# The last pair's drain, token tile 0 and the order of the output sums at the end of a decoder layer with MoE, on one core

## The reference

```python
x = x + g1[:, None, :] * (merged @ w_out[l])
h = modulate(rmsnorm(x, norm2[l]), sh2, sc2)
x = x + g2[:, None, :] * hier_moe(h, ...)
# hier_moe: each token goes to 2 of 32 experts, with weights e_w:
#   hid = silu(t @ w1) * (t @ w3) ; out += e_w * (hid @ w2)
```

## Time and profile before

| | us |
|---|---|
| median of 3 runs | 618.57 |
| lowest, highest | 617.46, 618.89 |
| profiled execution | 618.94 |
| its span | 617.1 |
| busy in the span: PE, DVE, ACT, POOL | 567.7, 303.4, 161.2, 118.8 |

### The profile page before, as it was taken

The page is one execution under the profiler, slowest core; times in us unless marked ns, Lnnn a source line. Parts: engine busy times, 40 slices in busy tenths (PEclk is TensorE's granted clock), DMA queues, the critical chain, the costliest instruction groups (busy, mean ns, idle before and its releaser), DMA issues.

```text
span 617.1 us, 7419 instructions
## 1 busy us (share of the span) xinstructions
PE 567.7 (92%) x2824; PEld 340.7 (55%) x2824; DVE 303.4 (49%) x579; ACT 161.2 (26%) x346; POOL 118.8 (19%) x162
## 2 busy tenths in 40 slices
PE   3889999999999999999999999999979868888894
PEld 1644787777666676788888864433323322233343
DVE  0228889556656466138854585432213202265147
ACT  3026040345333434346321301211112101112100
POOL 3022421089200002066000002111111101101000
PEclk9999999999999999999999999999989988889998
DMA  8996665520671507030697499999999999999963
GB/s 307 401 351 249 245 236 201 171 106 31 256 291 63 210 0 275 1 137 0 256 382 317 172 411 401 375 421 418 420 420 419 421 418 421 416 421 414 399 259 136
DMA packets 43768, 173.50 MB, mean 281 GB/s; under 512 B 6552, under 2 KB 6640, under 8 KB 32980
## 3 DMA queue, kind: packets, MB, share of 16 engines
q1 hardware_dynamic: 36288, 158.87, 65.0%
q0 software_dynamic: 5664, 12.51, 5.6%
q10 hardware_dynamic: 1780, 1.63, 0.8%
HBM read 164.86 MB, written 15.74 MB: 293 GB/s over the span
## 4 chain that ended last, share of the span: by engine, by line
PE 77%; DMA 11%; DVE 6%; issue 4%; SPq 1%; ACT 1%; POOL 0%; DVEq 0%; POOLq 0%; ACTq 0%
PE bank L1067 18%; PE bank L1104 8%; PE bank L724 5%; PE bank L726 5%; PE bank L725 5%; PE bank L713 4%; DMA late<-in_w_ada_dram 4%; DMA arena<-y_scratch 3%; DMA late<-in_w_in_dram 3%; PE bank L1035 2%; PE bank L717 2%; PE bank L719 2%; PE bank L907 2%; PE bank L718 2%; PE bank L909 2%
## 5 line engine op out<-in xcount | busy, mean ns | idle before, releaser
L1067 PE MATMUL bank<-arena,hT 128*64 128x512 f32 x320 | 79.7, 643 | 16.2 <-issue 15.3
L724 PE MATMUL bank<-hT_high,w_in_parts 128*128 128x512 f32 x160 | 66.3, 414 | 0.0
L726 PE MATMUL bank<-hT_high,w_in_parts 128*128 128x512 f32 x160 | 62.7, 392 | 0.0
L725 PE MATMUL bank<-hT_low,w_in_parts 128*128 128x512 f32 x160 | 62.4, 390 | 0.0
L1884 DVE SCALAR_TENSOR_TENSOR g1b<-g1b,bank 128x256 f32<-128x256 f32 x16 | 6.7, 421 | 108.2 <-ACT g1b L1407 108.2
L1067 PEld LDWEIGHTS bank<-arena,hT 128*64 128x64 f32 x320 | 24.8, 146 | 62.3 <-issue 61.3
L1067 PE MATMUL bank<-late,hT 128*64 128x512 f32 x160 | 37.9, 619 | 3.9 <-issue 3.9
L2219 POOL DMA_INDIRECT hT<-xn_scratch,gidx x14 | 15.9, 1134 | 110.4 <-PE bank L1035 94.4
L1413 ACT COPY g1b<-bank 128x256 f32<-128x256 f32 x16 | 6.0, 372 | 112.8 <-PE bank L1087 112.8
L1592 DVE TENSOR_REDUCE st<-bank 128x2 f32<-128x256 f32 (+3 forms) x16 | 13.2, 824 | 43.1 <-PE bank L750 43.1
L726 PEld LDWEIGHTS bank<-hT_high,w_in_parts 128*128 128x128 f32 x160 | 30.0, 188 | 6.7
(11 more groups left out here) (345 smaller groups left out, 1048.0 us busy)
## 6 DMA issues: line engine op xcount, KB each, us to landing
arena<-in_w_dram SPq DMA_DIRECT2D x48, 1024.0 KB, 23.7
late<-in_w_dram SPq DMA_DIRECT2D x28, 1024.0 KB, 26.7
late<-in_w_ada_dram SPq DMA_DIRECT2D x6, 2048.0 KB, 13.3
arena<-in_w_dram SPq DMA_DIRECT2D x24, 512.0 KB, 12.7
arena<-in_w_ada_dram SPq DMA_DIRECT2D x5, 2048.0 KB, 9.3
arena<-in_w_in_dram SPq DMA_DIRECT2D x4, 2048.0 KB, 7.5
late<-in_w_in_dram SPq DMA_DIRECT2D x4, 2048.0 KB, 15.8
y_scratch<-arena POOLq DMA_DIRECT2D x1, 4096.0 KB, 18.2
```

Source lines behind the costliest of these rows:

```text
L724: mm(bank[:, b, :], wH[:, b, k, :], hH[:, k, :], start=k == 0, stop=False)
L725: mm(bank[:, b, :], wH[:, b, k, :], hL[:, k, :], start=False, stop=False)
L726: last = mm(bank[:, b, :], wL[:, b, k, :], hH[:, k, :], start=False, stop=k == 7)
L1067: last = mm(bank[SLOTS * x:SLOTS * (x + 1), 2 + q % 2, :].rearrange("p (w f) -> p w f", w=2), xgT_of(q)[:, k, SLOTS * x:SLOTS * (x + 1)], ...
```

## The change

- SP reads the stored rows in the order of tiles 1, 0, 2, 3.
- In `step(15)` DVE now has only the first of tile 1's two sums. The first half of the last pair is drained behind it, then comes tile 1's second sum, then the second half's drain. Tile 2's two sums, before in `step(15)`, stand ahead of its first output now, as tile 3's do.
- DVE adds six outputs in the order n = 1, 5, 2, 6, 3, 7 (`OUT_ORDER`). Tile 0 (n = 0 and 4) is no longer among them: PE puts the residual rows into the two banks with an identity matrix (`first_tile`, one fp32 matmul of 512 columns for each half, opening the sum in the bank), and ACT copies the finished banks to `xs`, after which SP stores them.
- On PE the first of these matmuls stands in the middle of the last pair's `gate_up`, ahead of the wait for the second half of the weights. The second stands behind the last pair's `down`, and with it `spread(STORED, 4)`, which stood ahead of that `down`.
- The lines on `overflow` belong to a part that runs only where an expert has more than 64 tokens.

```diff
+        ROW_ORDER = (1, 0, 2, 3)
+        OUT_ORDER = (1, 5, 2, 6, 3, 7)
...
-            rows_of(range(TT))
+            rows_of(ROW_ORDER)
...
-            for n in range(2 * TT):
+            def store_out(n):
                 t, w = n % TT, slice(CH * (n // TT), CH * (n // TT + 1))
-                sp.wait_ge(out_ready, n + 1)
                 sp.dma_start(out_v[t][:, w], xs[:, t, w]).then_inc(out_stored, 16)
+
+            for i, n in enumerate(OUT_ORDER):
+                sp.wait_ge(out_ready, i + 1)
+                store_out(n)
+                if i in (1, 3):
+                    sp.wait_ge(exp_out, TILE0_COPIED + i // 2 + 1)
+                    store_out(TT * (i // 2))
...
+            def first_tile(h):
+
+                mm(bank[:, SPREAD_BANK[TT * h], :], ident[:, :], xs[:, 0, CH * h:CH * (h + 1)], start=True, stop=False)
...
                     if q == PAIRS - 1 and k == KT // 2:
+                        first_tile(0)
                         all_loaded()
...
-                              start=i == 0 and part == 0, stop=i == LAST - 1 and part == 1)
+                              start=i == 0 and part == 0 and t > 0, stop=i == LAST - 1 and part == 1)
...
             hidden_transposes(PAIRS - 1)
+            down(PAIRS - 1)
+            first_tile(1)
             spread(STORED, 4)
-            down(PAIRS - 1)
             spread(STORED, 5)
...
             for h in range(2):
                 y_high(1, h)
+            for h in range(2):
+                act.wait_ge(spread_done, TT * h + 1)
+                sc.copy(xs[:, 0, CH * h:CH * (h + 1)], bank[:, SPREAD_BANK[TT * h], :]).then_inc(exp_out, 1)
...
-                    for t in EARLY_ROWS:
-                        dve.wait_ge(yg_loaded[t], 16)
-                        add_stored(t)
+                    dve.wait_ge(yg_loaded[1], 16)
+                    add_stored(1, range(1))
...
-            for h in range(2):
-                drain_last(1, range(h, h + 1))
+            drain_last(1, range(1))
+            add_stored(1, range(1, 2))
+            drain_last(1, range(1, 2))
             for h in range(2):
                 y_low(1, h)
-            for n in range(2 * TT):
+            for n in OUT_ORDER:
                 t, w = n % TT, slice(CH * (n // TT), CH * (n // TT + 1))
-                if n < TT and t > EARLY_ROWS[-1]:
+                if t > 1 and n < TT:
                     dve.wait_ge(yg_loaded[t], 16)
                     add_stored(t)
                 dve.wait_ge(spread_done, n + 1)
```

More of the change, by code:

```diff
@@ L200, in hybrid_trunk @@
         LASTW = TT * PAIRS
-        EARLY_ROWS = range(1, 3)
+        ROW_ORDER = (1, 0, 2, 3)
+        OUT_ORDER = (1, 5, 2, 6, 3, 7)
         SPREAD_BANK = [2, 4, 0, 1, 3, 5, 6, 7]
@@ L463, in hybrid_trunk @@
         SMALL, LATE = 10, 6
+        TILE0_COPIED = 2
         def overflow_count(eng):
@@ L1167, in overflow @@
             def overflow(b):
+                pe.wait_ge(exp_out, TILE0_COPIED + 2)
                 pe.wait_ge(x_place, b + 1)
@@ L1921, in y_low, with add_stored @@
                     last.then_inc(yL_ready, 1)
-            def add_stored(t):
-                for j in range(2):
+            def add_stored(t, js=range(2)):
+                for j in js:
                     last = v.scalar_tensor_tensor(out=xs[:, t, :], in0=yg[:, t, j, :], scalar=cw[:, j, t:t + 1],
@@ L2090, in overflow_rows @@
             def overflow_rows():
-                dve.wait_ge(out_ready, 2 * TT)
+                dve.wait_ge(out_ready, len(OUT_ORDER))
+                dve.wait_ge(exp_out, TILE0_COPIED + 2)
                 dve.wait_ge(y2_loaded, 16 * TT)
```

## The result

| | us |
|---|---|
| median before, 20 runs | 618.86 (617.46 to 622.49) |
| median with the change, 20 runs | 622.80 (619.54 to 626.32) |
| ratio, 95% interval | 1.0059 (1.0044 to 1.0073) |
| profiled execution's span | 623.4 |

The change costs 0.59%, some 3.7 us (the two medians are 3.9 apart), where +1.2 us was forecast. The runs also spread more: 6.8 us between the extremes against 5.0, and already the fastest run is 2.1 us above the fastest one of before. That the scatter changes too is the first hint of what went wrong.

What follows compares the result with a forecast made beforehand. PE was to become the bound up to n = 5 at 606.95, then DVE's 8.37 us to 615.32 against 614.14, with 2.96 us to the span's end: +1.2 us on the median 618.57, 619.7; range 618.0 to 621.5.

Steps and rivals of the forecast that it cites:

- x: Start of the last pair's `gate_up` on PE; 583.06 in the profile that the prediction used.
- PE from the end of `down` to n = 5: PE's unbroken stream from 597.61 through tile 0's work and the spreads, ending at about 606.95.
- DVE behind n = 5: DVE's remaining outputs and four sums of tiles 2 and 3 from 606.95: 8.37 us, to 615.32.
- the rival of a falling clock: PE's spreads from 603.5 on run at 0.44 instead of 0.23: +2.9 us, 621.5; chance 0.08.
- Sum: End of the kernel: +1.2 us on the profiled execution, carried to the runs' median 618.57, giving 619.7.
- has time to spare: PE before the change: idles 1.78 us after tile 0's stored rows, then again before the last 18 matmuls at 604.95.
- the last weights (587.63): Landing that ends PE's 0.97 us wait in the last pair; the new kernel's end hangs on it through PE.
- The cover of `first_tile(0)`: PE's wait for weights (586.66 to 587.63) hides this 0.86 us matmul, with 0.1 us left.
- the weights land earlier: Rival: `first_tile(0)` stands bare on PE's path, +0.86 us on top, 620.6; chance 0.04.
- The one on the faster side: Rival: later scattered reads, by up to 2.05 us, hurt only the kernel before; 617.7 at 2.05; chance 0.10.
- The claim that the profiled execution is an ordinary one: Argument against the reads rival: the profiled execution is not faster than the median, so its reads were hardly early.
- The drains 5 us earlier: DVE's drains before the spreads: last pair's parts ready at about 600.5 instead of 605.55.

Runs made afterwards that it cites:

- c2_before: Kernel before, unedited, one run for another profile: 618.59 us.
- c0_before: Kernel before, unedited, measured again for a second profile: ratio 1.0005, span 617.6 us.
- x_before_pe_late: Kernel before plus two dummy fp32 matmuls on PE right behind the last pair's `down`: ratio 1.0004.
- a_drains_only: Kernel before plus the earlier drains, new read order and tile 2's sums behind `y_low`; tile 0 still finished by DVE: ratio 1.0013.
- a_tile0_only: Kernel before plus tile 0 finished by `first_tile` and ACT's copies, with the drains, reads and early sums of before: ratio 1.0029.
- b_both: Changed kernel with all tile 0 work last on PE, tile 2's sums ahead of DVE's first output, outputs 1, 2, 5, 6, 3, 7: ratio 0.9963.
- c4_before: Kernel before, unedited, one run for another profile: 618.77 us.

## Why the prediction was wrong

**The sum from x on held.** From x to DVE's last output it had 615.32 - 583.06 = 32.26 us; the four profiles of the changed kernel have 32.08 to 32.13. PE from the end of `down` to n = 5: 9.34 predicted, 9.17 found (603.19 to 612.36). DVE behind n = 5: 8.37 and 8.36. The clock: no window from 588 to PE's end below 1.00, as forecast; the rival of a falling clock in that stretch did not happen. From DVE's last output to the span's end it is 2.65 us, 0.3 less than I kept.

**What failed is "Sum": "+1.2 us against the profiled execution ..., carried over to the median of the runs", with "the sum is good to some 0.6 us either way".** x = 583.06 was taken as fixed. It is a draw: over all 18 profiles of these kernels it lies between 583.06 and 589.05, and the one that I had is the lowest. For the kernel before that could not be seen, since its end hardly depends on x: DVE's four sums, tied to the reads, ended at 602.7 to 604.2 (with the two dummy matmuls too), while x went over 5.7 us. The prediction noted that PE "has time to spare" (it idles 1.78 and 0.65 us ahead of the last spreads) and that the change takes it, but put no price on the spare time as a cover for PE's scatter. It also tied the new kernel's end to the last weights (587.63); in the changed kernel's profile PE does not wait for them at all, and the chain goes back to the wait ahead of pair 14's `gate_up`.

With the mean x of the four profiles of before, 585.6, the same sum gives 585.6 + 32.1 = 617.7 against a mean DVE end of 614.2: +3.5 us. Measured were +3.7 (0.59% of 618.86). That the two agree to 0.2 us is partly luck: a mean of four draws with a scatter of over 2 us is good to about 1 us only.

**The first profile was unusual at its end too.** Its reads were the earliest of the four (DVE's sums start at 597.48, in the others at 598.10 to 598.92), but its last spreads ran at the lower clock and took 6.00 us for 18 records. In c2_before they take 4.38, at a granted clock of 1.00:

```profile
605.57 4.38 PE L1131 MATMUL bank<-y_parts,slot_to_token 128*128 128x512 f32 x18 [0.65 <-DVE y_parts L1918]
```

Behind its four sums DVE needed 11.4 us to its end in the first profile and 10.5 to 10.6 in the others. Early reads and slow spreads about cancelled, which is one more reason why its end looked ordinary.

**Where x comes from** shows in the same profiles, three things that add up. Pair 14's `gate_up` starts between 570.1 and 572.9, behind a wait that is for its weights in the code; the profile names nothing for it ("issue"). Its 32 records take 7.09 or 8.78 us (seven and eleven of the 18 profiles), by whether the clock fell behind that wait. And `down` behind it takes 3.65 or 5.35 us (thirteen and five). The first profile of before had the earliest start and both short forms. The changed kernel's granted clock behind the two waits (the column after POOL's):

```profile
573.00:574.00 1.00, 1.00 (x6) 0.47 (x4) 0.00 (x0) 0.00 (x0) 0.00 (x0) 0.75 0.98 397
574.00:575.00 1.00, 1.00 (x4) 0.30 (x2) 0.00 (x0) 0.00 (x0) 0.00 (x0) 0.50 1.00 381
...
584.00:585.00 1.00, 1.00 (x6) 0.32 (x4) 0.00 (x0) 0.00 (x0) 0.00 (x0) 0.50 0.99 406
```

**The cover of `first_tile(0)`.** Costed at nothing, with the weights' landing named as its cover and "up to 0.86" without it. In the changed kernel's profile PE did not wait for weights there, and it stood bare: from 592.15 to 593.21, 1.06 us. The rival named it ("the weights land earlier"), but had the cause the wrong way round: the weights do not come earlier, PE comes later. It does not change the 32.1 us, as in the first profile the wait for weights had the same length.

**The rivals' weight.** The one on the faster side argued from the reads' scatter that before could be the one that suffers. The scatter on PE's side, which decides for the new kernel, was not asked about, and it is the larger. The claim that the profiled execution is an ordinary one, because its time is near the median, holds only for what ends last in it.

**The drains 5 us earlier** were right as a mechanism and mostly gone too: at x = 588.6 the first drain waits 2.31 us for PE, and the parts were ready at 605.8, no earlier than in the first profile of before (605.55). At the same x (c0_before) the kernel before has them at 607.0, so 1.2 us of the gain are left.

**Does the change move x itself?** Nothing shows that it does. The four profiles of the changed kernel have a mean of 587.7, those of before 585.6. But PE's work up to x is the same in all variants, and over all 18 profiles the difference is gone: the six of the kernel before and of its variants (x_before_pe_late, a_drains_only) have a mean of 586.1, the twelve of the changed kernel and of its variants 586.1 as well. The runs agree: the changed kernel's median of 622.80, less the 1.8 us that a time is longer than its span, 2.7 from DVE's end to the span's end and 32.1, leaves an x of 586.2. With x = 586.1 the sum gives +4.0 us. (The six runs beside the variants, with a median of 624.49, give 587.9.) A shift of up to about 1 us stays possible within this scatter.

**Left open**: why the first tile 0 variant alone (a_tile0_only) lost 1.4 us more than its profile's distances give at a middling x, and why the second measurement of the changed kernel came out at 1.0090, six runs of which any number may be late draws of x.

## To carry to other kernels

An engine that idles a few us ahead of a join (the point where another engine waits for it) is not free to be loaded: its idle time may be what absorbs its own scatter from one execution to the next, and the time of the old kernel doesn't show that scatter. Before costing work into such a gap, profile the kernel several times and read when that engine arrives, or load it with a dummy of known length and see what the end does. Work whose result is needed last, by an engine that has nothing else to do, belongs at the end of the producer's stream. Ahead of the join the two dummy matmuls cost their full 1.7 us; at the end, tile 0's work of 7.0 us (603.95 to 610.98) reached only 1.5 us beyond DVE's last output (b_both).

## What was not expected of the hardware

PE's clock behind an idle time varies from one execution to the next at the same place of the same program. Ahead of pair 14's `gate_up`, with 1.12 to 1.29 us of idling it never fell (four profiles); with 3.39 to 3.51 it fell in two of five; with 3.71 to 3.94 in all nine. A fall costs 1.7 us (8.78 against 7.09 for 32 records). Two profiles of the kernel before, c2_before and c4_before, side by side:

```profile
571.44 7.09 PE L1067 MATMUL bank<-late,hT 128*64 128x512 f32 x32 [3.51 <-issue]
571.65 8.78 PE L1067 MATMUL bank<-late,hT 128*64 128x512 f32 x32 [3.44 <-issue]
```

Ahead of `down` the idle times are the same in all profiles (1.39 and 0.46), and it fell in five of 18. The Trainium skill (TensorE: Matmul & The Clock Gate, "What's actually happening") has the level set by recent activity; the rows agree with that, and show that two executions of one program can differ in level at the same place.
